# Adaptive modulation in slabs of 128 features, in four column groups of TensorE, with the first value products between the slabs

## What is computed

```python
def _modulation(cvec, w_ada, b_ada):
    m = jax.nn.silu(cvec) @ w_ada + b_ada
    return m[..., :D_MODEL], m[..., D_MODEL:2 * D_MODEL], m[..., 2 * D_MODEL:]

def _project(x, shift, scale, w_in):
    h = _rmsnorm(x) * (1.0 + scale) + shift
    p = h @ w_in
```

## Time and profile before

| | us |
|---|---|
| median of 3 runs (1123.71 to 1124.89) | 1124.06 |
| the profiled execution's own time | 1125.86 |
| its span | 1124.0 |
| PE busy in the span | 1074.1 (96%) |
| DVE busy | 785.8 (70%) |
| ACT busy | 567.7 (51%) |
| POOL busy | 103.0 (9%) |

### The profile page before, as it was taken

How to read it: one execution, slowest core, us unless ns; L and a number is a source line. 1 busy time by engine, 2 the same in 40 slices (tenths; PEclk the granted TensorE clock), 3 DMA queues, 4 the chain that set the end, 5 groups by cost and what they waited for, 6 DMA issues and landing times.

```text
span 1124.0 us, 18333 instructions
## 1 busy us (share of the span) xinstructions
PE 1074.1 (96%) x6459; PEld 938.9 (84%) x6459; DVE 785.8 (70%) x1559; ACT 567.7 (51%) x1051; POOL 103.0 (9%) x115
## 2 busy tenths in 40 slices
PE   7899999999999999999999999899998779999997
PEld 1799988988888988888888888788887769898896
DVE  6778668867876876776788688678698566445443
ACT  5842246645663664565677577477477432121111
POOL 0000100000000000000000000000001343352430
PEclk9999999999999999999999999999999999999999
DMA  9824637973884797399499299488399875353630
GB/s 360 311 100 127 203 109 143 181 211 70 169 183 124 154 184 195 77 182 238 121 186 178 77 187 182 136 175 169 98 198 239 241 262 168 133 175 108 202 131 38
DMA packets 320271, 188.99 MB, mean 168 GB/s; under 512 B 256182, under 2 KB 299190, under 8 KB 320188
## 3 DMA queue, kind: packets, MB, share of 16 engines
q1 hardware_dynamic: 306364, 165.97, 60.2%
q10 hardware_dynamic: 13824, 21.96, 6.3%
HBM read 94.27 MB, written 32.78 MB: 113 GB/s over the span
## 4 chain that ended last, share of the span: by engine, by line
PE 59%; DVE 14%; DMA 11%; ACT 6%; SPq 5%; issue 4%; POOL 0%; DVEq 0%; ACTq 0%
PE d_ps_pairs L108 14%; PE s_ps_pairs L108 10%; PE y_ps L2197 9%; PE b_ps L108 9%; PE o_ps_pairs L1063 5%; PE v_ps L108 4%; DMA xl<-pl 4%; DVE pl L1756 3%; SPq L1187 3%; DVE mn L1679 3%; ACT ph L1462 2%; ACT pr L1442 2%; DMA gt<-gates_d 2%; DMA x<-in_w_ada 2%; PE s_ps_pairs L1313 1%
## 5 line engine op out<-in xcount | busy, mean ns | idle before, releaser
L108 PE MATMUL d_ps_pairs<-h,wt 128*128 128x384 f32 (+4 forms) x1848 | 353.5, 347 | 4.1 <-ACT craw L1480 3.4
L108 PEld LDWEIGHTS d_ps_pairs<-h,wt 128*128 128x128 f32 x1848 | 320.2, 189 | 27.1 <-issue 6.2
L108 PE MATMUL s_ps_pairs<-h,wt 128*128 128x512 f32 (+1 forms) x864 | 171.6, 356 | 1.7 <-DVE q L1639 1.4
L1442 ACT ACTIVATE pr<-s_ps_pairs,mx 128x896 f32<-128x896 f32 (+1 forms) x128 | 124.7, 977 | 74.6 <-DVE mx L1701 74.2
L108 PEld LDWEIGHTS s_ps_pairs<-h,wt 128*128 128x128 f32 x864 | 141.6, 189 | 23.8 <-DVE q L1639 1.6
L1756 DVE SCALAR_TENSOR_TENSOR pl<-pr,rden,ph 128x896 f16<-128x896 f32 (+1 forms) x128 | 140.1, 1116 | 27.1 <-DMA xl<-pl 19.4
L1462 ACT ACTIVATE ph<-pr,rden 128x896 f16<-128x896 f32 (+1 forms) x128 | 125.0, 1011 | 15.5 <-DVE rden L1737 6.7
L2197 PE MATMUL y_ps<-wo,mg 128*128 128x512 f32 (+1 forms) x504 | 115.9, 390 | 6.5 <-DVE wo L1888 4.5
L2197 PEld LDWEIGHTS y_ps<-wo,mg 128*128 128x128 f32 x504 | 92.0, 191 | 29.0 <-issue 6.2
L1679 DVE TENSOR_REDUCE mn<-s_ps_pairs 128x2 f32<-128x1024 f32 x64 | 78.1, 1221 | 25.0 <-PE s_ps_pairs L1316 21.7
L108 PE MATMUL b_ps<-og,wb 128*128 128x256 f32 x720 | 88.3, 283 | 4.4 <-DVE wb L1888 4.3
(11 more groups left out here) (241 smaller groups left out, 1634.2 us busy)
## 6 DMA issues: line engine op xcount, KB each, us to landing
wraw<-in_w_gate SPq DMA_DIRECT2D x24, 512.0 KB, 4.4
gt<-gates_d SPq DMA_DIRECT2D x40, 256.0 KB, 4.6
wada<-in_w_ada SPq DMA_DIRECT2D x12, 512.0 KB, 7.6
gates_d<-craw ACTq DMA_DIRECT2D x30, 192.0 KB, 3.0
oz<-gates_d SPq DMA_DIRECT2D x20, 256.0 KB, 4.9
oz<-o_d SPq DMA_DIRECT2D x20, 256.0 KB, 3.9
x_f<-in_x SPq DMA_DIRECT2D x10, 512.0 KB, 6.6
y<-y_f SPq DMA_DIRECT2D x9, 512.0 KB, 2.7
```

Source lines behind the costliest of these rows:

```text
L108: mm = eng.matmul(out, lhs(a, k), rhs(b, k), start=(k == 0 and i == 0), stop=(k == n_k - 1 and i == 2))
L1442: act.activation(probs_run(s, t, pb * STEPS + s), scores_run(s, t), ACT.Exp, bias=mx[:, t:t + 1], scale=-1.0, accum_out=den[:, t:t + 1]).t ...
```

## The change

w_ada's shift and scale thirds are stored on the host as eight slabs: slab k holds, for the 128 features of block k, all 1024 rows of shift and scale (1 MB, 8 row blocks x 256 columns). After one slab the shift and scale of these 128 features are complete. `modulation(k)` takes a slab in plain fp32: row block b is a matmul of 32 stationary columns (two conditioning vectors and 30 of zeros, `cpad`) whose output goes to PSUM partitions 32 (b % 4) on, so four matmuls address four column groups of the array, and the next four add to them. ACT copies the 128 x 256 out (`mod_rows`), `columns(k)` sums the four groups and turns them into columns by a matmul with a 0/1 matrix `sel`, and `modf_of(k)` adds the biases. No part of the slabs is split any more.

x tiles 0 to 3 are loaded ahead of or between the slabs. The first half of the values of tiles 0 to 3 (four units, four PSUM banks) accumulates over the feature blocks while slabs arrive (`first_values`). The keys of tiles 0 to 3 run as one group of 512 behind it. The second half of the values' weights comes later into unused parts of `h`, and is split after the first phase. The order of chunks alternates between group 0 and 1. From value unit 8 on, the order is that of before.

```diff
-    modrow = [h32[0:4, :, :], x1[0:4, 2:3, :].rearrange("p o (c n) -> p (o c) n", c=2)]
+    sel = left["sel"]
+    rows = [hm_raw[:, 1, k, 832:1088] for k in range(KD)]
+    cpad = hm_raw[:, 1, :, 1088:1120]
...
-    CHUNK = [(g, k) for g in range(NX) for k in range(KD)]
+    CHUNK = ([(g, k) for g in range(2) for k in range(2)] + [(g, k) for k in range(2, KD) for g in range(2)]
+             + [(g, k) for g in range(2, NX) for k in range(KD)])
...
+    FIRST_TILES = 4
+    UNITS_V = [(t, n) for n in range(2) for t in range(FIRST_TILES)] + [(t, n) for t in range(FIRST_TILES, TT) for n in range(2)]
...
-    RING = 8
-    SHIFT, SCALE, KEYS, VALUES = 0, 8, 16, 17
...
+    RING = 4
+    COLS = 2 * P
...
+    def slab(k):
+        s = k % RING
+        ap = wada[:, 2 * s:2 * s + 2, :] if s < RING - 1 else x2[:, :, :]
+        return ap.rearrange("p a d -> p (a d)").rearrange("p (b c) -> p b c", c=COLS)
+    def first_values_raw(j):
+        return hm_raw[:, 0, 2 * j:2 * j + 2, 512:512 + HW]
+    def keys_raw(j):
+        return hm_raw[:, 0, 2 * j:2 * j + 2, 512 + HW:512 + HW + P]
+    def keys_split(j, part):
+        return wkb[:, part, 2 * j * P:(2 * j + 2) * P].rearrange("p (k c) -> p k c", c=P)
+    def values_raw(m):
+        k0, nk = VK[m]
+        return hm_raw[:, 1, k0:k0 + nk, 512:512 + HW]
+    def values_split(k0, nk, n, part):
+        return wv[:, part, k0:k0 + nk, n * HW:(n + 1) * HW]
...
+        def load_slab(k):
+            if k >= RING:
+                sp.wait_ge(mod_mm, k - RING + 1)
+            sp.dma_start(slab(k), io["w_mod"][k]).then_inc(slab_in[k % RING], 16)
+        def load_values_keys(j):
+            sp.dma_start(hm_raw[:, 0, 2 * j:2 * j + 2, 512:512 + HW + P], io["w_vk"][:, 2 * j:2 * j + 2, :]
+                         ).then_inc(vk_in[j], 16)
+        def load_values(m):
+            k0, nk = VK[m]
+            sp.wait_ge(wk_hi, m + 1)
+            sp.dma_start(values_raw(m), io["w_vl"][:, k0:k0 + nk, :]).then_inc(vk_in[m], 16)
...
+        sp.dma_start(sel[:, :], io["sel"]).then_inc(small_in, 16)
+        load_first_x()
         sp.dma_start(ident[:, :], io["ident"]).then_inc(ident_in, 16)
-        for k in range(4, KD):
-            load_ada(0, k)
-        for k in range(KD - 1):
-            load_ada(1, k)
-        load_first_x()
-        load_ada(1, KD - 1)
-        load_keys()
-        for m in range(3):
-            load_v(m)
+        load_slab(0)
+        load_values_keys(0)
+        load_slab(1)
         load_x(1)
-        for m in range(3, 6):
-            load_v(m)
-        sp.wait_ge(sq_done, XG[0][1])
-        sp.wait_ge(mod_col, 2)
+        load_slab(2)
+        load_values_keys(1)
+        load_slab(3)
+        load_slab(4)
+        load_values_keys(2)
+        load_slab(5)
+        load_slab(6)
+        load_values_keys(3)
+        load_slab(7)
+        sp.wait_ge(sq_done, FIRST_TILES)
         load_x(2)
-        sp.wait_ge(wk_lo, 2)
-        sp.wait_ge(wv_lo, 6)
+        for m in range(len(VK)):
+            load_values(m)
+        sp.wait_ge(mod_mm, KD)
...
+        def modulation(k):
+            pe.wait_ge(slab_in[k % RING], 16 * (k // RING + 1))
             for b in range(KD):
-                if b % 4 == 0:
-                    pe.wait_ge(mod_row, 2 * half + b // 4 + 1)
-                mm = pe.transpose((mod_ps, k_ps)[half][:, 4 * b:4 * b + 4], modrow[half][:, b // 4, (b % 4) * P:(b % 4 + 1) * P],
-                                  ident[0:4, 0:4])
+                r = slice(32 * (b % 4), 32 * (b % 4) + 32)
+                mm = pe.matmul(mod_ps[r, 0:COLS], cpad[:, b, :], slab(k)[:, b, :], start=(b < 4), stop=(b >= 4))
+            mm.then_inc(mod_mm, 1)
+        def columns(k):
+            pe.wait_ge(mod_row, k + 1)
+            if k > 0:
+                pe.wait_ge(mod_ready, 2 * k)
+            for half in range(2):
+                c0 = 4 * k + 2 * half
+                mm = pe.matmul(k_ps[:, c0:c0 + 2], rows[k][:, half * P:(half + 1) * P], sel[:, :], start=True, stop=True)
             mm.then_inc(mod_col, 1)
...
+        def first_values(g, k):
+            t0, n = XG[g]
+            pe.wait_ge(lo_done, CHUNK.index((g, k)) + 1)
+            pe.wait_ge(wv_lo, k // 2 + 1)
+            for t in range(t0, t0 + n):
+                for i, (a, b) in enumerate(((0, 0), (0, 1), (1, 0))):
+                    mm = pe.matmul(v_ps[:, t, 0:HW], hm[:, a, k, t * P:(t + 1) * P], wv[:, b, k, 0:HW],
+                                   start=(k == 0 and i == 0), stop=(k == KD - 1 and i == 2))
+                if k == KD - 1:
+                    mm.then_inc(mm_done, 1)
...
+            pe.wait_ge(lo_done, KD * max([t0 <= t < t0 + tn for t0, tn in XG].index(True) + 1, 2))
+            pe.wait_ge(v_hi, u - 3)
+            for m, (k0, nk) in enumerate(VK):
+                if u == FIRST_TILES:
+                    pe.wait_ge(wv_lo, KD // 2 + m + 1)
+                mm = split_mm(pe, v_ps[:, u % 4, 0:HW], lambda a, k: hm[:, a, k, t * P:(t + 1) * P],
+                              lambda b, k: wv[:, b, k, n * HW:(n + 1) * HW], KD, k0, k0 + nk)
+            mm.then_inc(mm_done, 1)
...
-        pe.wait_ge(scl_done, 2)
-        pe.wait_ge(const_set, 1)
-        for half, k in MODS:
-            modulation(half, k)
         pe.wait_ge(ident_in, 16)
-        columns(0)
         transposed(0)
         transposed(1)
+        pe.wait_ge(silu_done, 2)
+        pe.wait_ge(small_in, 48)
+        modulation(0)
+        columns(0)
+        modulation(1)
+        first_values(0, 0)
         columns(1)
+        first_values(0, 1)
+        modulation(2)
         transposed(2)
+        transposed(3)
+        columns(2)
+        first_values(1, 0)
+        first_values(1, 1)
+        transposed(4)
+        transposed(5)
+        for k in range(2, KD):
+            if k + 1 < KD:
+                modulation(k + 1)
+            first_values(0, k)
+            if k + 1 < KD:
+                columns(k + 1)
+                transposed(2 * (k + 1))
+            first_values(1, k)
+            if k + 1 < KD:
+                transposed(2 * (k + 1) + 1)
         for k in range(KD):
-            if k + 3 < KD:
-                transposed(k + 3)
-            if k == 0:
-                pe.wait_ge(wk_lo, 1)
-            if k == KD // 2:
-                pe.wait_ge(wk_lo, 2)
             keys_chunk(0, k)
-        value_unit(0)
-        value_unit(1)
-        for j in range(2):
-            for c in range(3):
-                transposed(KD + 3 * j + c)
-            value_unit(2 + j)
-        pe.wait_ge(k_raw, 1)
-        for k in range(KD):
-            if k + 6 < KD:
-                transposed(KD + k + 6)
-            keys_chunk(1, k)
         value_unit(4)
...
+        def mod_rows(k):
+            act.wait_ge(mod_mm, k + 1)
+            act.activation(rows[k], mod_ps[:, 0:COLS], ACT.Copy).then_inc(mod_row, 1)
...
+        mod_rows(0)
+        first_values_high(0)
+        modulate(0)
+        mod_rows(1)
+        modulate(1)
+        square(1, 0)
         root(1)
+        keys_high(0)
+        mod_rows(2)
+        modulate(2)
+        modulate(3)
+        for k in range(2, KD):
+            if k > 2:
+                mod_rows(k)
+            if k % 2 == 0:
+                first_values_high(k // 2)
+            modulate(2 * k)
+            modulate(2 * k + 1)
+            if k % 2 == 0:
+                keys_high(k // 2)
+        for u in range(FIRST_TILES):
+            value(u)
+        for t in range(XG[2][1]):
+            square(2, t)
+        root(2)
+        for m in range(len(VK)):
+            values_high(m)
         keys(0)
...
+        def modf_of(k):
+            dve.wait_ge(small_in, 48)
+            dve.wait_ge(mod_col, k + 1)
+            dve.tensor_scalar(modf[:, k, :], k_ps[:, 4 * k:4 * k + 2], bcol[:, k:k + 1], None, ALU.add).then_inc(mod_ready, 1)
+            dve.tensor_scalar(modf[:, KD + k, :], k_ps[:, 4 * k + 2:4 * k + 4], bcol[:, KD + k:KD + k + 1], 1.0, ALU.add,
+                              ALU.add).then_inc(mod_ready, 1)
...
+        modf_of(0)
+        first_values_low(0)
+        parts(0)
+        modf_of(1)
+        parts(1)
+        square_too(3, x_in[1])
+        normalise(1)
         keys_low(0)
+        modf_of(2)
+        parts(2)
+        parts(3)
+        for k in range(2, KD):
+            if k > 2:
+                modf_of(k)
+            if k % 2 == 0:
+                first_values_low(k // 2)
+            parts(2 * k)
+            parts(2 * k + 1)
+            if k % 2 == 0:
+                keys_low(k // 2)
+        for u in range(FIRST_TILES):
+            value(u)
+        normalise(2)
+        for m in range(len(VK)):
             values_low(m)
         value(4)
...
+    a["w_mod"] = ada[:, :2 * D].reshape(KD, P, 2, KD, P).transpose(3, 1, 0, 2, 4).reshape(KD, P, KD, 2 * P)
+    a["sel"] = (np.arange(P)[:, None] % 32 == np.arange(2)[None]).astype(np.float32)
...
```

(65 more changed lines are left out.)

263 lines of the change are left out of this document (74 added, 189 removed).

## The result

| | before | changed |
|---|---|---|
| median of 9 runs each, us | 1124.06 (1120.43 to 1125.39) | 1132.28 (1127.84 to 1136.04) |
| profiled execution, its span | 1125.86, 1124.0 | 1128.87, 1127.0 |

The ratio is 1.0074, 95% interval 1.0055 to 1.0092: slower by 8.2 us. The profiled execution of the changed kernel lies 3.4 us under its median and that of before 1.8 us over its own, so the two traces differ by 3.0 us only.

What follows compares the result with a forecast made beforehand. TensorE was taken to bound the kernel from 41 us on; phase end 53.8 plus 36.4 put value unit 8's end at about 90.1 against 86.7, and +3.4 on the median 1124.06 gave 1127.5 us, range 1118.5 to 1131.5.

Steps and rivals of the forecast that it cites:

- The slab, 2.0 us: TensorE's modulation products for one slab of 128 features: 16 records in 9 slots of 0.22 us, 2.0 us.
- if PE starts records in order, B-high can start with A-low and B-low only behind B-high: Within a slab, two fp32 products' high and low records on their column groups: only two run at a time, 2.0 us.
- One k: TensorE work for one feature block in the first phase's loop: slab, values, columns and transposes, 4.6 us.
- Half rate only until 14.8: Cold start: PE's first records, slab 0's modulation, take 3.57 us at half rate from 11.4 to 14.8 us.
- First phase ends at 53.8: End of the loop over slabs with the first values of tiles 0 to 3, at 53.8 us.
- The wait of 4.0 us: PE stands 4.0 us between keys and value unit 4, for the late split of the second half of the value weights.
- Keys and the work from there to the mark: Stretch from the first phase's end through keys and value units to the end of value unit 8: 36.4 us.
- The clock's fall in the wait: Worse form: PE's clock falls to half during its stand before value unit 4, +1.7 us, giving 1129.2.
- The mark +3.4: End of value unit 8 (tile 4, first half) at 90.1 us against 86.7 before, +3.4 us.
- Whatever shift the mark gets, the rest should get too: Everything behind the end of value unit 8 moves by that unit's shift, +3.4 us, to the kernel's end.
- DMA not the bound: First phase: TensorE's 4.6 us per feature block sets the pace, above the 3.2 us in which 1.3 MB lands.
- Rival B: Four column groups run at once: 1.0 us a slab, phase ends at 47.4, wait stays; shift -3.0, 1121.0 us; chance 29%.

Runs made afterwards that it cites:

- e9: Changed kernel with each column group's two products of a slab sent in succession; 1128.15 us in one run, against 1124.68 for the kernel before.
- e6: Changed kernel with all eight products of a slab sent to one column group; 1154.25 us in one run, against 1124.68 for the kernel before.
- e8: Changed kernel with constant products on PE at the start and in the first phase's waits; 1126.32 us, ratio 1.0013 to the kernel before.
- The square: Changed kernel, second-half weight splits late or early: shifts against before +7.1 and +1.8 us with clock left alone, +1.6 and -3.2 with front kept busy.
- e4: Changed kernel with 16 products of 512 columns put into the wait before value unit 4; 1127.88 us, ratio 1.0033 to the kernel before.
- e10: The kernel before, unchanged, traced a second time; that execution took 1123.61 us.
- e3: Changed kernel with 28 constant products on PE ahead of the first transposes only; 1129.36 us, ratio 1.0044 to the kernel before.
- e7: Changed kernel with constant products at the start and in the first phase's waits, and second-half weight splits moved early; 1121.53 us, ratio 0.9973 to before.

## Why the prediction was wrong

The forecast was 1127.5 and the range ended at 1131.5; the median was 1132.28. The sign was right, the size was not, and two terms of the sum were wrong in opposite ways: the slab was half as dear, and the clock, which the sum had at full from 14.8 us on, was not. Of the 4.8 us missed in the median, 1.4 are in the first trace's own time: its phase ends 1.7 early, the half clock behind the wait adds 2.4, and under 1 us comes behind. The other 3.4 lie in slower executions, and their cause stays open.

- **The slab, 2.0 us: failed.** It takes 1.00. The failing step is "if PE starts records in order, B-high can start with A-low and B-low only behind B-high". I had the row that speaks for running side by side and discounted it by an argument about two records on one group that no row showed. e9 shows that argument to be false, e6 that without groups it would be 3.57. One k was 3.79 against 4.6. The Trainium skill ("TensorE: Matmul & The Clock Gate", Part 3) gives 2.38 times for three column groups, and the estimate from it, 1.1 us a slab, was near. The same part of the Trainium skill says that matmuls start and end in program order; by my reading of it e9's slab would take 2.8 us, and it takes 1.02, so either the rule does not hold between column groups or the records do not stand in the order of the products, and the measurement decides for the price.
- **Half rate only until 14.8: failed.** "PE's first records run at half rate as at 5.56": in the front of before matmuls follow each other up to 30 us with one wait of 1.23 us and a few of 0.2, the new one is small pieces with waits of 0.5 to 2.0 us between. It was half rate until 26.2, or full from 14.1 or 18.1 and down again at 21. modulation(3) started at 30.29, 28.33 and 29.07 against 28.3, even though three slabs ahead of it were cheaper than I had them; with the clock kept it starts at 27.12 (e8). So the traces price this term at 1.2 to 3.2 us where the forecast had 1.4, for slab 0 alone (even its 3.4 for this slab is short of 2.0 at the rate of its own rows, 3.8). The square prices the filling at 5.0 to 5.5 us in the median, with 2.5 to 3 of error and with what lies behind the mark in it.
- **First phase ends at 53.8:** 52.12, 50.16, 50.91. With the right slab and the clock kept it ends at 48.95 (e8), 4.9 us ahead of the forecast; the cold clock gives 1.2 to 3.2 us of that back. Two errors thus cancel in part, and that the end is within 4 us of the forecast is luck.
- **The wait of 4.0 us: right**, in size, releaser and cause, in every trace with the order unchanged (3.98 to 4.01). Keys and the work from there to the mark were right too, as e4's 36.5 against 36.4 shows.
- **The clock's fall in the wait:** named as a worse form at +1.7 and left out of the sum. It is there each time the wait is without work in it, at 2.4 us (e4 against the first trace), 1.5 in e8. It belonged in the sum: the row at 5.56 shows half rate behind idle time, and nothing spoke against it.
- **The mark +3.4:** +4.4 in the first pair, +3.7 to +4.9 and +3.1 against e10.
- **"Whatever shift the mark gets, the rest should get too": failed.** 0.3 to 1.8 us more by 208 and 2 to 4 more by 538, of which 2 to 4 come back. At the end of the traces it is +4.2 to +5.7 against e10.
- **DMA not the bound: right** for the change, where PE waits for no slab, and by little: it waits 0.2 to 0.5 us once the clock is kept, and 1.03 in e3.
- **Rival B** had the slab right, and the wait of 4.0. e8 comes nearest to what it supposes, with full clock in the front and the wait in place: its mark is at 87.02 where B's sum has 83.7, 1.5 us of it from the phase's end (48.95 against 47.4) and 1.5 from half clock behind the wait, and its shift is +1.6 and not -3.0. That e7's 1121.53 stands beside B's 1121.0 is a coincidence, since e7 has no wait.

What stays open: the three traces of the change took 1127.84 to 1129.33 us, while the medians of the same kernel's runs are 1132.28 and 1130.61. Some 2 to 4 us of the loss are thus in executions that no trace shows. That the cold front varies between executions is seen; that it makes these 2 to 4 us is not shown, and the spread speaks against its being the whole: with the clock kept in the front, the runs of e8 and e7 still spread over 5.7 and 5.9 us, and their medians lie 1.5 and 2.6 us above their traces. The square shows what lowers the medians, not where in those executions the time goes.

## What to carry to other kernels

When work moves from one dense block into the gaps of a dependent chain, price it at the clock it will have there, and ask of every new wait what runs at half rate behind it: here, by the medians, taking both away turned a loss of 7 us into a gain of 3. Before discounting a row that shows tiles running side by side, look for a row that shows the reason for the discount. And when the order of two engines makes a third wait while all inputs have landed, move those steps first: four lines of order were worth 5 us.
